# Expert results stored by indices, with the rows of empty slots skipped and their memory filled once in the projection stage

## The reference

```
g_sel  = argmax(ut @ w_rg + b_rg)                      # 1 of 4 groups
e_prob = softmax((ut @ w_re + b_re)[g_sel])            # 8 experts of the group
top_p, top_i = top_k(e_prob, 2)                        # 2 experts for each token
hid = silu(ut @ w_gate[e]) * (ut @ w_up[e]) * combine  # 2048 -> 256
out = sum over the two experts of hid @ w_down[e]      # 256 -> 2048
y   = h + out
```

## Time and profile before

| | |
|---|---|
| median of three runs | 2513.96 us (2502.53 to 2514.57) |
| the profiled execution, its own time | 2518.48 us |
| its span, first to last instruction | 2516.7 us |
| mean granted TensorE clock | 0.902 |
| TensorE busy | 2105.9 us, 84% |
| VectorE, ScalarE, GpSimd busy | 520.6, 245.9, 108.3 us |
| moved by the DMA engines | 614.82 MB, mean 244 GB/s |
| of it by q1, q0, q10 | 545.19, 45.07, 22.55 MB |

### The profile page before, as it was taken

The page is one execution under the profiler, slowest core; times in us unless marked ns, Lnnn a source line. Parts: engine busy times, 40 slices in busy tenths (PEclk is TensorE's granted clock), DMA queues, the critical chain, the costliest instruction groups (busy, mean ns, idle before and its releaser), DMA issues. The chain is left out here.

```text
span 2516.7 us, 33756 instructions
## 1 busy us (share of the span) xinstructions
PE 2105.9 (84%) x13731; PEld 1291.3 (51%) x13731; DVE 520.6 (21%) x1079; ACT 245.9 (10%) x646; POOL 108.3 (4%) x124
## 2 busy tenths in 40 slices
PE   7999999999599999977788777999983677777763
PEld 7887677777376666654344443774331232332321
DVE  2553000046620221211112111110013011111112
ACT  0001100012101221110001001000010000000000
POOL 0000000000000000000000000000001121221211
PEclk8999999989769999988888898999995788898886
DMA  7665533322423322239999998642338999999998
GB/s 251 201 180 184 183 117 119 131 84 84 154 77 116 99 97 97 95 108 404 413 413 412 407 409 329 246 151 104 113 126 330 383 403 405 398 414 403 375 417 340
DMA packets 149395, 614.82 MB, mean 244 GB/s; under 512 B 31765, under 2 KB 68902, under 8 KB 111590
## 3 DMA queue, kind: packets, MB, share of 16 engines
q1 hardware_dynamic: 107166, 545.19, 55.5%
q0 software_dynamic: 22800, 45.07, 5.0%
q10 hardware_dynamic: 19288, 22.55, 2.8%
HBM read 702.95 MB, written 39.60 MB: 295 GB/s over the span
## 5 line engine op out<-in xcount | busy, mean ns | idle before, releaser
L480 PE MATMUL bank<-ut,wring 128*128 128x320 f32 x1408 | 384.7, 435 | 1.1 <-PEq L193 1.1
L480 PEld LDWEIGHTS bank<-ut,wring 128*128 128x128 f32 x1408 | 268.3, 191 | 112.4 <-issue 4.0
L740 PE MATMUL bank<-ut,wring 128*128 128x320 f32 x1024 | 309.9, 450 | 16.8 <-ACT selmask L903 15.0
L740 PEld LDWEIGHTS bank<-ut,wring 128*128 128x128 f32 x1024 | 195.1, 197 | 95.6 <-issue 30.8
L1990 PE MATMUL bank<-wdn,par 128*32 128x512 f32 x512 | 87.7, 817 | 116.2 <-issue 112.8
L608 DVE RECIPROCAL snew<-snew 128x320 f32<-128x320 f32 x30 | 64.5, 2149 | 279.4 <-ACT snew L583 279.4
L1432 PE MATMUL bank<-wring,arena 128*128 128x512 f32 x256 | 118.4, 605 | 3.1 <-DVE arena L1469 1.6
L1961 PE MATMUL bank<-wgu,arena 128*32 128x512 f32 x1024 | 120.0, 609 | 0.8 <-DVE arena L2041 0.8
L1990 PEld LDWEIGHTS bank<-wdn,par 128*32 128x32 f32 x512 | 18.0, 132 | 148.5 <-issue 144.6
L1331 DVE TENSOR_REDUCE wring<-bank 128x1 f32<-128x512 f32 x32 | 22.1, 692 | 312.6 <-PE bank L1153 312.6
L2062 DVE COPY arena<-bank 128x512 f32<-128x512 f32 x52 | 36.0, 692 | 234.7 <-PE bank L1990 234.7
(11 more groups left out here) (412 smaller groups left out, 2340.2 us busy)
## 6 DMA issues: line engine op xcount, KB each, us to landing
wgu<-in_w_gu SPq DMA_DIRECT2D x128, 1024.0 KB, 16.5
wdn<-in_w_dn SPq DMA_DIRECT2D x32, 2048.0 KB, 25.7
wring<-in_w_proj SPq DMA_DIRECT2D x44, 1024.0 KB, 4.8
arena<-in_kv_k SPq DMA_DIRECT2D x64, 640.0 KB, 9.6
arena<-in_kv_v SPq DMA_DIRECT2D x64, 640.0 KB, 16.3
wring<-in_w_gate SPq DMA_DIRECT2D x32, 1024.0 KB, 5.1
wring<-in_w_merge SPq DMA_DIRECT2D x32, 1024.0 KB, 4.8
wring<-in_kv_k SPq DMA_DIRECT2D x32, 640.0 KB, 15.5
```

The costliest lines, as they stand in the source:

```text
L480: last = nc.tensor.matmul(m.bank[:, 2 + s % 2, 0:T], m.wring[:, s, k * P:(k + 1) * P], m.ut[:, k, :], start=(k == 0), stop=(k == KD - 1))
L740: last = nc.tensor.matmul(m.bank[:, 6 + n % 2, 0:T], m.wring[:, n % 3, k * P:(k + 1) * P], m.ut[:, k, :], start=(k == 0), stop=(k == KD - 1))
```

## The change

The expert stage's stores from gpsimd become indirect: each of the 128 partitions goes to the row of `y_slot` (cut into quarters of 512 numbers) that an index names, and the index of an untaken slot is made larger than the bound, so that nothing is written for it. The indices are computed once: four small loads bring the slots' tokens into `y_tok`, with the slots of a tile down 32 partitions, four times; VectorE turns "no token" into 2^20 and adds the row number `y_row`, a constant that is loaded in routing. The last two tiles keep their direct stores. The memory of `y_slot` is filled once, with rows of `w_merge`, by four copies from memory to memory behind gpsimd's two cache copies in the projection. The wait for the filling of `slot_token` moves from a semaphore of its own to the shared one of the stores, and the expert stage's `add_step` is renamed to `dve_step` and counts from 2 higher.

```diff
@@ -466,7 +466,10 @@
                 pool.dma_start(a["o_" + name].rearrange("b (c e) -> b c e", e=1024),
                                a["old_" + name][:, NT * G * P:WIN * G * P].rearrange("b (c e) -> b c e", e=1024)
                                ).then_inc(cv_kept, 16)
-            pool.wait_ge(cv_kept, 32)
+            for c in range(4):
+                at = slice(c * SLOTS_E // 4, (c + 1) * SLOTS_E // 4)
+                pool.dma_start(a["y_slot"][at, :], a["w_merge"].rearrange("n p d -> (n p) d")[at, :]).then_inc(cv_kept, 16)
+            pool.wait_ge(cv_kept, 96)
 
         @block.tensor
         def _(pe):
@@ -1394,14 +1397,14 @@
             for i in range(2):
                 load_gates(i)
             sp.dma_start(m.flat[:, KD * T:2 * KD * T], a["x_tok"]).then_inc(x_in, 16)
-            sp.dma_start(a["slot_token"], a["no_token"]).then_inc(tok_in, 16)
+            sp.dma_start(a["slot_token"], a["no_token"]).then_inc(m.stores, 16)
             for n in range(SLOTS, NW):
                 sp.wait_ge(tile_done, n - SLOTS + 1)
                 sp.dma_start(m.wring[:, n % SLOTS, :], a["w_merge"][n, :, :]).then_inc(m.w_in[n % SLOTS], 16)
                 if n in (2 * GJ, 3 * GJ):
                     sp.wait_ge(sig_ready, n - GJ)
                     load_gates(n // GJ)
-            sp.wait_ge(tok_in, 16)
+            sp.wait_ge(m.stores, 7 * 16)
 
         @block.tensor
         def _(pe):
@@ -1489,7 +1492,7 @@
 GU = KD * 2 * FF
 DN = 2 * DM
 E_LAYOUT = [("fold", P), ("tri2", P), ("stack", TW), ("slot0", NE), ("past", NE), ("upto", NE * NE), ("over", NOV),
-            ("before", EPG * EPG), ("nth", NX), ("row", 1), ("half", 1)]
+            ("before", EPG * EPG), ("nth", NX), ("row", 1), ("half", 1), ("y_row", NTILE)]
 E_AT = {}
 _at = 0
 for _name, _n in E_LAYOUT:
@@ -1532,6 +1535,8 @@
         self.w_hi, self.w_lo = sb("w_hi", P, 3), sb("w_lo", P, 3)
         self.w_at = sb("w_at", P, NX, dt=I32)
         self.tok_at = sb("tok_at", P, NGRP, dt=I32)
+        self.y_tok, self.y_at = sb("y_tok", P, NTILE, dt=I32), sb("y_at", P, NTILE, dt=I32)
+        self.y_row, self.y_none = sb("y_row", P, NTILE), sb("y_none", P, NTILE)
         self.un = m.flat[:, 0:KD * T]
         self.xg = m.flat[:, 0:DM]
         self.ut_x = m.flat[:, DM:2 * DM].rearrange("p (k t) -> p k t", k=KD)
@@ -1600,6 +1605,8 @@
             sp.dma_start(e.token_id[:, :], a["token_id"]).then_inc(r_in, 16)
             at, n = E_AT["stack"]
             sp.dma_start(e.stack[:, :], a["e_consts"][:, at:at + n]).then_inc(moved, 16)
+            at, n = E_AT["y_row"]
+            sp.dma_start(e.y_row[:, :], a["e_consts"][:, at:at + n]).then_inc(moved, 16)
             for n in range(2):
                 load_base(sp, e, a, n)
 
@@ -1834,7 +1841,7 @@
             sem("gu_done"), sem("part_ready"), sem("st_done"), sem("silu_ready"), sem("hid_ready"))
         dn_done, y_ready, y_free, back_in = (
             sem("dn_done"), sem("y_ready"), [sem(f"y_free{s}") for s in range(NY)], [sem(f"back_in{b}") for b in range(3)])
-        add_step, gu_free = sem("add_step"), sem("gu_free")
+        dve_step, gu_free, y_tok_in = sem("dve_step"), sem("gu_free"), sem("y_tok_in")
         back = e.wgu[:, :, :, :].rearrange("p s k n -> p (s k n)")
         got = [[back[:, (2 * b + j) * DM:(2 * b + j + 1) * DM] for j in range(2)] for b in range(2)]
         got.append([back[:, 4 * DM + j * 1024:4 * DM + (j + 1) * 1024] for j in range(2)])
@@ -1900,11 +1907,19 @@
 
             def store(j):
                 pool.wait_ge(y_ready, j + 1)
-                pool.dma_start(a["y_slot"][TILE_OF[j] * TW:(TILE_OF[j] + 1) * TW, :].rearrange(
-                    "t (j n) -> j t n", j=4), e.yt[j % NY]).then_inc(y_free[j % NY], 16)
+                if j == 0:
+                    pool.wait_ge(dve_step, 2)
+                n = TILE_OF[j]
+                pool.indirect_dma_start(out=a["y_slot"].rearrange("r (j n) -> (r j) n", j=4),
+                                        out_offset=bass.IndirectOffsetOnAxis(ap=e.y_at[:, n:n + 1], axis=0),
+                                        in_=e.yt[j % NY], in_offset=None, bounds_check=4 * SLOTS_E - 1,
+                                        oob_is_err=False).then_inc(y_free[j % NY], 16)
 
             gather(0)
             load_gu(0)
+            for j in range(4):
+                pool.dma_start(e.y_tok[j * TW:(j + 1) * TW, :], a["slot_token"].rearrange("(n t) o -> t (n o)", t=TW),
+                               allow_slow_non_contiguous=True).then_inc(y_tok_in, 16)
             n = 1
             for i, (kind, x) in enumerate(ORDER):
                 while n < NGRP and FIRST_USE[GROUPS[n - 1]] <= i + 1:
@@ -2047,6 +2062,12 @@
                 while n < NGRP and FIRST_USE[GROUPS[n]] <= i + 1:
                     keep(n)
                     n += 1
+                if i == 2:
+                    dve.wait_ge(y_tok_in, 64)
+                    nc.vector.tensor_scalar(e.y_none[:, :], e.y_tok[:, :], T - 0.5, float(1 << 20), ALU.is_gt, ALU.mult
+                                            ).then_inc(dve_step, 1)
+                    dve.wait_ge(dve_step, 1)
+                    nc.vector.tensor_tensor(e.y_at[:, :], e.y_none[:, :], e.y_row[:, :], ALU.add).then_inc(dve_step, 1)
                 if 1 <= i <= NTILE:
                     j = i - 1
                     dve.wait_ge(silu_ready, j + 1)
@@ -2147,6 +2168,7 @@
     c["before"] = np.broadcast_to((g[None, :] < g[:, None]).reshape(1, -1), (P, EPG * EPG))
     c["nth"] = np.broadcast_to(np.arange(NX) + 0.5, (P, NX))
     c["row"], c["half"] = p[:, None], (p // 64 - 2)[:, None]
+    c["y_row"] = np.arange(NTILE)[None, :] * P + (p % TW * 4 + p // TW)[:, None]
     return np.ascontiguousarray(np.concatenate([np.asarray(c[n]).reshape(P, w) for n, w in E_LAYOUT], axis=1),
                                 dtype=np.float32)
 
```

More of the change, by code:

```diff
@@ L1380, in merge_stage @@
             sem("x_in"), sem("tile_done"), sem("sig_ready"), sem("mix_ready"), sem("h_ready"), sem("dve_step"))
-        ss_ready, tok_in = sem("ss_ready"), sem("tok_in")
+        ss_ready = sem("ss_ready")
         g_in = [sem(f"g_in{s}") for s in range(2)]
@@ L1657, in _ @@
             nc.scalar.activation(ev[:, :, :], ev[:, :, :], ACT.Exp).then_inc(exp_done, 1)
-            act.wait_ge(moved, 96)
+            act.wait_ge(moved, 112)
         @block.tensor
@@ L1869, in _ @@
             for b in range(3):
-                sp.wait_ge(add_step, 2 * b + 2)
+                sp.wait_ge(dve_step, 2 * b + 4)
                 cols = slice(b * DM, (b + 1) * DM if b < 2 else KD * T)
                 sp.dma_start(a["y_tok"][:, cols], hb[:, cols]).then_inc(m.stores, 16)
-            sp.wait_ge(m.stores, 9 * 16)
+            sp.wait_ge(m.stores, 10 * 16)
         @block.gpsimd
@@ L2068, in _ @@
                     if j:
-                        dve.wait_ge(add_step, 2 * b + 1)
+                        dve.wait_ge(dve_step, 2 * b + 3)
                     hv = hb01[:, b, :] if b < 2 else hb[:, 2 * DM:KD * T]
                     nc.vector.scalar_tensor_tensor(out=hv, in0=got[b][j], scalar=w[:, b:b + 1], in1=hv, op0=ALU.mult,
-                                                   op1=ALU.add).then_inc(add_step, 1)
+                                                   op1=ALU.add).then_inc(dve_step, 1)
 def layer_program(nc, a):
```

## The result

The changed kernel takes 2523.77 us in the median (2519.32 to 2529.17, 8 runs), the kernel before 2508.05 us in the same comparison (2500.46 to 2514.57, 8 runs): ratio 1.0057, with a 95% interval of 1.0039 to 1.0075. It is slower by 15.7 us, where +34 us and 2548 us were forecast; 2523.77 lies inside the outer range of 2520 to 2568, and outside the forecast's own of 2535 to 2560. Run once more beside other kernels it took 2526.45 against 2509.4 us (ratio 1.0066, 1.0040 to 1.0092).

The account below looks back on a forecast made before the run. The prediction took TensorE to bound the projection and DMA bandwidth the expert stage. Projection +37.8 and experts -4 made +34 us, giving 2548 us from a median of 2513.96; range 2520 to 2568, the forecast's own 2535 to 2560.

Parts of the forecast that it names:

- It has 14 to 15 turns to go beside the filling: Projection: cos table's slowest engine alternates with 2.67 us filling pieces, landing at 301.2 us; TensorE 35.3 late, +37.8 with clock.
- a start of the small product before 285 us: Projection: sign of a wrong forecast; TensorE's product needing w_small and the cos table was forecast near 301 us, not 266.
- The clock behind the wait: Projection: after its long wait TensorE resumes at a lower clock, adding 2.5 us.
- Turns: Expert stage: a scatter's 8 packets per engine, against a store's 4, delay token gathers on q0; +8 us, bounds 0 to 26.
- Rival B: Expert stage: 200 more turns per engine on q0 make gathers late; +15 instead of -4, 2567 us, chance 0.12.
- The y_tok loads: Expert stage: four small loads stand in q0 ahead of an awaited gather; 1 us each, +4, bounds 0 to 14.8.
- Bytes and skipped rows: Expert stage: 8.2 MB fewer stored saves 20.3 us if bandwidth alone binds; 4000 skipped pieces cost 4.2 us.
- The sum of the stage: Expert stage: -20.3 + 4.2 + 4 + 8 = -4 us, bounds -20 to +25.
- Rival C: Expert stage: the whole bandwidth gain comes through, -17 instead of -4; with the stall 2535 us, chance 0.12.
- The base: Whole kernel: the median before the change, 2513.96 us, from which 2548 us was forecast.
- Rival A: Projection: filling hidden, only the expert stage changes, by -4 to -17; 2497 to 2510 us, say 2505, chance 0.12.
- the prediction's passage on the fit: Projection: the skill's 2.0 us plus bytes by 436 GB/s gives the filling 31 us, present copies 21, where 32.6 were measured.

Follow-up runs that it names:

- e1: The kernel before with only the four filling copies added, stores still direct; 2539.76 us against 2511.19, ratio 1.0121.
- e11: The changed kernel run once more, unchanged, against the kernel before; 2526.45 us, ratio 1.0066.
- e9: The changed kernel with the filling as one copy in pieces of 32 KB; 2529.85 us, ratio 1.0077 to the kernel before.
- e10: The kernel before with its 50 stores made indexed, every row written, no filling, no y_tok loads; 2503.87 us, ratio 0.9981.
- e3: The changed kernel without the filling and with no row skipped, y_tok loads kept; 2509.5 us, ratio 1.0004 to the kernel before.
- e5: The kernel before with the four y_tok loads added on gpsimd's queue, values unused, stores direct; 2518.22 us, ratio 1.0044.
- e8: The changed kernel with 8 KB filling pieces and the y_tok loads on ScalarE's queue at the expert stage's start; 2489.41 us, ratio 0.9928.
- e2: The changed kernel with the filling in pieces of 8 KB, same bytes; 2497.5 us, ratio 0.9952 to the kernel before.

## Why the prediction was wrong

Its sign and its place held, and so did the mechanism of the stall: loads that take turns with large pieces. The number of those turns was wrong, and with it the largest term. In the expert stage the forecast's mechanism of turns was wrong in sign and two more terms were off; that their sum came within 6 us of the measured one is luck.

1. **"It has 14 to 15 turns to go beside the filling", +37.8: the step that failed.** Measured +25 and +30 in the projection (28.6 us for the filling alone, by e1's times). The table was forecast for 301 us, 71.9 after the stage's start, and came 48.0 after it (52.9 in e11). `w_small` was forecast at 60 to 72 us and landed after 32.1, hardly later than before (31.5). The forecast named a start of the small product before 285 us as the sign that it is wrong: it started at 274.11.
Two errors make the number of turns. I took the worst engine from the landing of a weight tile, 27.0 us. That landing does not tell when the table lands: it was 18.5 us in the changed kernel, 24.4 in e1 and 27.8 in e9, and the table took 46.7, 51.7 and 44.6. And I gave every turn the length of a large piece, which leaves out the crowd of tiny packets at the copies' end, 6 turns per engine in 2.2 us. q1 had sent 399 packets by 256.8 us, as the earlier trace rows has it, so 177 of the 576 were left, 11 per engine; 96 went with the crowd. The remaining 81, 5 per engine at 18 x 16 / 115 = 2.5 us a turn, give 12.7 us from 259 on: 271.7, against 274.1 measured. In e11 the same count (402 by 257 us, 90 in the next 2.2, then 108 packets of q0 in 17 us) gives 272 against 279.0, so the average engine isn't quite enough there. The landings say it without a count: `w_small` was there at 259.0, at the crowd's end, and the table 15.1 us later (19.3 in e11), which is 6 to 8 turns. The turn's length was forecast well (2.67), and so was the end of the filling (305; its last copy landed at 305.2); the number of turns beside large pieces was not. The count explains the size; no run took the tiny packets away to test it.
Tile 4 then needs 144 packets, 9 turns, of 20 x 16 / 146 = 2.2 us: 20 us, and it came 20.4 after the table. I had let it follow within 6 us, since the filling was to be over at 305. This error goes the other way, and is why the first one did not cost more.

2. **The clock behind the wait, +2.5 (within the +37.8):** 2.3 and 2.6 us. The size was right for one wait, but there were two.

3. **"Turns", +8:** wrong in sign. The scatter's form is worth -7 to -9 by the stages of e10 against before and e1 (591.8 and 589.9), about -5 by e10's run times, and -12 by e3 against e5. Two counts were wrong. I had given the scatter 8 packets per engine where the direct store has 4; it has 4 as well (64 per store in e10), so there are no extra turns. And I had counted a store's packets between 2 and 8 KB only, 4 per engine, and called the small ones skipped rows of the weight gathers. Half of them were the direct stores' own: 12 per engine and store, and each stood in q0 ahead of the next gather. Rival B (+15, 2567 us) rested on the same count and falls with it: the stage got shorter.

4. **The y_tok loads, +4:** 7 to 12 us (e5: +10 to +12; the changed kernel's stage, 581.5 to 582.4, against e8's 572.2; e3 against e10, 7.5). Each landed after 18.8 us in the median, not 3.7. It was inside the bounds, 0 to 14.8, and the truth lay nearer to the upper one: the loads stand in q0 right ahead of the gather for which TensorE waits.

5. **Bytes and skipped rows, -20.3 + 4.2 = -16:** -8 to -10 (e3's 590.1 against 582; e10's 582.6 against e8's 572.2). The bytes did go: on the whole q0 moves 50.55 MB, 5.48 more than before, which is the filling's 13.63 less 8.15. Worth per byte they were half of what bandwidth gives. Why, stays open: the skipped rows add tiny packets (11,314 against e10's 9296, half of the 4000 that I had counted), and the DMA share of the stretch is 0.97 with fewer bytes per us; no run separates the two.

6. **The sum of the stage, -4:** -9.5, made of about -10 (form), -9 (rows skipped) and +10 (loads). Of the forecast's own parts none was near; the total was, by luck. Rival C, the whole bandwidth gain (-17), did not come.

7. **The base.** 2548 stands on a median of 2513.96 from three runs; eight gave 2508.05. That is 6 of the 24 us by which it was too high.

The rule of the Trainium skill (DMA: Bandwidth & Descriptors, SWDGE vs HWDGE vs iDMA) that a packet is preferably at most 4096 B did not describe these copies: in the 18 us from 262 on q0 moved 5.17 MB in 115 packets, 45 KB each on average with the tiny ones among them. No run used pieces of 4 KB; at 8 KB the stall was already gone (e2). Rival A, hidden filling, came true only there, where its condition, small pieces, was met (2497.5 us, in its range of 2497 to 2510). In the prediction's passage on the fit, 31 us leaves out the fixed part that the 21 us beside it contains; with it the filling would take 33 us. It took 46, from about 259 to 305.2, where 42.7 were forecast.

Not tried: the changed stores with the filling left out altogether.

## What to carry to other kernels

Beside a stream of large pieces on one queue, another queue moved its own packet size for each of them; work out that rate (here 8 KB per piece) and hold it against what the consumer uses, and where it is less, cut the pieces or start them when the consumer's buffers are full. When you count what is queued, count the tiny packets too, both as turns taken from a queue and as turns given to the other. Take small loads from the queue ahead of a gather that is waited for: onto another queue, and early.

## What was not expected of the hardware

- The two cache copies sent 288 packets on q0 for their 128 pieces: 160 tiny ones, 72 by 241 us, as they began, and 88 after 259, as they ended. Through those at the end the other queue got 96 packets in 2.2 us. The copies of the filling, also 64 pieces each, sent only 16 tiny ones each (608 packets on q0 in all). Why the cache copies have more stays open.
- A direct store of 128 x 512 numbers from gpsimd leaves about 190 packets under 512 B; the indexed store of the same rows leaves none of these, sends its 128 rows of 2 KB as 64 packets of 4 KB, as the direct store does, and lands after 9.7 us instead of 20.5, with the same bytes.
- Cutting pieces from 53 to 32 KB changed nothing clear of the spread (478.6 to 487.4 us over four profiles against 481.6), to 16 KB gave 461.1, to 8 KB 454.4.
